# Loads, warm products and the first scale row at the start of a hybrid gMLP, GLA and PEER trunk

## The reference

```python
def rmsnorm(x, g):
    xf = x.astype(jnp.float32)
    y = xf * lax.rsqrt(jnp.mean(xf * xf, axis=-1, keepdims=True) + NORM_EPS)
    return (y * g.astype(jnp.float32)).astype(x.dtype)

def mixer_a(h, w_in, b_in, ln_g, ln_b, w_s, b_s, w_out):
    z = jax.nn.gelu(h @ w_in + b_in, approximate=False)   # w_in: 1024 x 4096
    ...
```

## Time and profile before

| | |
|---|---|
| Median of 3 runs | 1977.58 us (1977.37 to 1978.27) |
| The profiled execution | 1977.18 us |
| Its span in the profile | 1975.5 us |
| TensorE busy | 1939.1 us (98%) |
| VectorE busy | 1348.2 us (68%) |
| ScalarE busy | 1071.4 us (54%) |
| GpSimd busy | 271.4 us (14%) |
| Memory traffic | 338.82 MB, mean 172 GB/s |

### The profile page before, as it was taken

One profiled execution on the slowest core, in us unless ns is written; L12 is line 12 of the kernel. 1 busy time (PEld: TensorE's weight loads), 2 busy tenths in 40 slices (PEclk: granted clock), 3 DMA queues, 4 the chain that ended last, 5 costly groups with the idle time before them and its releaser, 6 DMA issues.

```text
span 1975.5 us, 39160 instructions
## 1 busy us (share of the span) xinstructions
PE 1939.1 (98%) x12636; PEld 1768.9 (90%) x12636; DVE 1348.2 (68%) x2319; ACT 1071.4 (54%) x1864; POOL 271.4 (14%) x122
## 2 busy tenths in 40 slices
PE   7989999999999999999999999999999999999998
PEld 6878999999999888888888799999999998888887
DVE  5774859478888666666658649575888876666666
ACT  4535444566666555445565544445666665544554
POOL 0113770200000000000006068420000000000000
PEclk9999999999999999999999999999999999999999
DMA  7744455544444555555554344555444445555554
GB/s 259 240 138 153 150 188 181 182 158 138 138 138 139 191 191 193 194 195 192 191 167 133 127 151 163 184 185 181 139 138 138 140 158 192 193 193 195 194 191 149
DMA packets 92806, 338.82 MB, mean 172 GB/s; under 512 B 10384, under 2 KB 10512, under 8 KB 92240
## 3 DMA queue, kind: packets, MB, share of 16 engines
q1 hardware_dynamic: 90864, 329.49, 50.0%
q0 software_dynamic: 1888, 8.62, 1.3%
HBM read 337.02 MB, written 1.05 MB: 171 GB/s over the span
## 4 chain that ended last, share of the span: by engine, by line
PE 87%; POOL 4%; issue 4%; DVE 3%; ACT 1%; DMA 0%; POOLq 0%; DVEq 0%; ACTq 0%
PE psum L1079 86%; POOL tile_lo L369 4%; DVE tile_lo L702 1%; ACT tile_hi L440 1%; DVE zv L803 0%; DVE qe L1017 0%; DMA gain_row<-in_gains 0%; DVE zu L812 0%; DVE ke L1018 0%; ACT hT_hi L475 0%; DVE hn L752 0%; DVE zu L777 0%; DVE score_in L1029 0%; DVE x L736 0%; DVE yT_lo L818 0%
## 5 line engine op out<-in xcount | busy, mean ns | idle before, releaser
L702 DVE TENSOR_TENSOR tile_lo<-raw,tile_hi 128x1024 fp32r<-128x1024 f32 x548 | 676.6, 1235 | 295.0 <-ACT tile_hi L440 294.6
L440 ACT ACTIVATE tile_hi<-raw 128x1024 fp32r<-128x1024 f32 x624 | 655.5, 1051 | 349.5 <-PE psum L1079 348.9
L1079 PE MATMUL psum<-hT_hi,tile_hi 128*128 128x256 f32 x2368 | 591.3, 289 | 3.8 <-ACT hT_hi L475 2.7
L1079 PE MATMUL psum<-hT_lo,tile_hi 128*128 128x256 f32 x2368 | 577.2, 283 | 0.0
L1079 PEld LDWEIGHTS psum<-hT_hi,tile_hi 128*128 128x128 f32 x2368 | 451.2, 191 | 5.8 <-ACT hT_hi L475 3.4
L1079 PEld LDWEIGHTS psum<-hT_lo,tile_hi 128*128 128x128 f32 x2368 | 451.9, 191 | 0.0
L1079 PE MATMUL psum<-hT_hi,tile_lo 128*128 128x256 f32 x2368 | 332.9, 283 | 3.7 <-POOL tile_lo L369 3.7
L1079 PEld LDWEIGHTS psum<-hT_hi,tile_lo 128*128 128x128 f32 x2368 | 305.3, 192 | 4.9 <-POOL tile_lo L369 4.9
L580 ACT ACTIVATE w_hi<-acts 128x256 fp32r (+1 forms) x256 | 106.8, 418 | 341.7 <-PE psum L1079 341.0
L1079 PE MATMUL psum<-tile_lo,w_hi 128*128 128x512 f32 x1024 | 274.9, 389 | 0.0
L1079 PE MATMUL psum<-tile_hi,w_lo 128*128 128x512 f32 x1024 | 274.7, 389 | 0.0
(11 more groups left out here) (184 smaller groups left out, 1365.4 us busy)
## 6 DMA issues: line engine op xcount, KB each, us to landing
raw<-in_u SPq DMA_DIRECT2D x256, 512.0 KB, 3.3
raw<-in_v SPq DMA_DIRECT2D x256, 512.0 KB, 3.3
raw<-in_a_in SPq DMA_DIRECT2D x32, 512.0 KB, 4.5
raw<-in_w_q SPq DMA_DIRECT2D x32, 512.0 KB, 3.3
raw<-in_a_out SPq DMA_DIRECT2D x16, 512.0 KB, 3.2
raw<-in_b_rv SPq DMA_DIRECT2D x16, 512.0 KB, 3.3
raw<-in_b_qk SPq DMA_DIRECT2D x8, 512.0 KB, 3.2
raw<-in_b_out SPq DMA_DIRECT2D x8, 512.0 KB, 3.3
```

The costliest lines, as they stand in the source:

```text
L440: act.activation(tile_hi[slot % SPLIT_SLOTS][:, :], raw[slot][:, :], ACT.Copy).then_inc(hi_ready, 1)
L702: dve.tensor_tensor(tile_lo[s][:, :], raw[slot][:, :], tile_hi[s][:, :].bitcast(F32), ALU.subtract).then_inc(lo_ready, 1)
L1079: return pe.matmul(o, a, b, start=start, stop=stop, skip_group_check=True)
```

## The change

It has four parts. The request for the first gain row moves from GpSimd to ScalarE, ahead of its norm. SyncE waits until both halves of x have landed before it requests tiles 0 and 1, requests tile 2 when tile 0 has landed, and tile 3 when tile 1 has. GpSimd, in the place of the gain row, fills the block from which warm products read with zeros. TensorE, before it waits for the constants, runs 72 products of this block with itself into a PSUM bank that is used later.

```diff
@@ -75,6 +75,7 @@
 RAW_SLOTS = 4
 SPLIT_SLOTS = 2
 WARM = 28
+WARM_FIRST = 72
 LOWEST = -3.0e38
 
 
@@ -226,6 +227,7 @@
         raw_loaded = [sem(f"raw_loaded{s}") for s in range(RAW_SLOTS)]
         hi_ready, lo_ready, tile_used = sem("hi_ready"), sem("lo_ready"), sem("tile_used")
         numbers_ready = sem("numbers_ready")
+        warm_ready = sem("warm_ready")
         consts_loaded = sem("consts_loaded")
         x_loaded = [sem(f"x_loaded{h}") for h in range(TT)]
         gain_loaded = [sem(f"gain_loaded{i}") for i in range(5)]
@@ -311,7 +313,11 @@
                         sp.wait_ge(made, i * RAW_SLOTS + (count + s - start))
                         load(t[name][i * RAW_SLOTS + s], s)
 
+            for h in range(TT):
+                sp.wait_ge(x_loaded[h], 16)
             for s in range(RAW_SLOTS):
+                if s >= SPLIT_SLOTS:
+                    sp.wait_ge(raw_loaded[s - SPLIT_SLOTS], 16)
                 load(t["a_in"][s], s)
             stage("a_in", AIN, RAW_SLOTS, N_AIN)
             stage("a_out", AOUT, 0, N_AOUT)
@@ -344,7 +350,7 @@
                     pool.wait_ge(free, count)
                 pool.dma_start(gain_row[:, :], t["gains"][i].partition_broadcast(P)).then_inc(gain_loaded[i], 16)
 
-            load_gain(0, None, 0)
+            pool.memset(numbers16[:, 0:P // GROUP, :], 0.0).then_inc(warm_ready, 1)
 
             pool.wait_ge(hn_ready[0], 1)
             pool.dma_start(b_in[:, 0:A_WIDTH], t["b_in"][0:A_WIDTH].partition_broadcast(P)).then_inc(b_in_loaded[0], 16)
@@ -476,6 +482,7 @@
                                    psum[:, 4 + b, :].rearrange("p (a b) -> p a b", a=4), ACT.Copy).then_inc(hT_hi_ready[i], 1)
 
 
+            act.dma_start(gain_row[:, :], t["gains"][0].partition_broadcast(P)).then_inc(gain_loaded[0], 16)
             norm(0, 0, 1)
 
             def a_gelu(j, h):
@@ -1174,6 +1181,9 @@
 
 
             warm = numbers16[:, 0:P // GROUP, :].rearrange("p a b -> p (a b)")
+            pe.wait_ge(warm_ready, 1)
+            for c in range(WARM_FIRST):
+                product(psum[:, 4, 0:P], warm, warm, start=True, stop=True)
             pe.wait_ge(consts_loaded, 16)
             norm(0)
             for j in range(A_BLOCKS):
```

## The result

The changed kernel takes 1980.87 us (median of 18 executions, 1978.98 to 1983.8), the kernel before in the same series 1978.32 (18 executions, 1977.33 to 1979.9): +2.55 us, a ratio of 1.0014 with a 95% interval of 1.0007 to 1.002. The interval leaves out 1, so the change is slower, but by less than the 0.2% that the prediction set as its bound for no change. The profiled execution took 1979.51 us, with a span of 1977.8 (before 1975.5).

A forecast was written before the change was run, and what follows sets the result against it. The prediction took TensorE's stream as bound, its start set by gain row and weight tile 1's landing. Conversion 1 0.86 us later, other parts 0, summed to +0.9 us: 1978.5 us by the median, range 1975.6 to 1981.1.

The forecast's parts named there:

- the 0.2% that the prediction set as its bound for no change: Whole kernel: a measurement can tell about 0.2%, 4.0 us, from no change; chance of staying within it 0.91.
- The start is bound twice: Before the product stream: gain row and weight tile 1's landing both bind, without slack; removing the 1.95 us gain-row wait leaves the other.
- The second x was to lie 1.5 us later: Start transfers: sharing engines with the gain row delays second x by 1.3 to 1.8 us, middle 1.5, to 7.0 us.
- Tile 0 was to land 3.2 us after its request: First weight tile on SyncE's queue: requested at 7.05 us, landing 3.2 us later as a tile alone does, at 10.25.
- The 1.3 us from tile 0 to tile 1: Weight transfers: tile 1's bytes follow tile 0's, so it lands 1.3 us later, at 11.55 us.
- the rival 5%: TensorE idles before first products, stays at 1.2 GHz into the stream, 2.7 us more a tile; 1983.9 us; chance 5%.
- Against: the first products of before came after a 4.4 us run of work begun cold and were already quick: Stream's start on TensorE: argument against the rival of a slower clock, which cost 2.7 us a tile; chance 5%.
- The 72 products were hidden: TensorE before the transposes: warm products take 4.5 to 8.9 us, covered; value taken 0, bounds 0 to 0.2 us gained.
- b_in had 0 in the sum: GpSimd's bias-row transfer beside tile 1: counted 0; rival 1.3 to 2.6 us more, 1979.8 to 1981.1 us, chance 13%.
- x near 7.0: Sign in the profile after: the second x lands near 7.0 us, not 5.5.
- conversion 1 near 11.5: Sign in the profile after: ScalarE's conversion of weight tile 1 begins at its landing, near 11.5 us.
- the stream at 16.0: Sign on TensorE: the stream of products begins near 16.0 us instead of 15.18, later stretches the same, shifted.

The follow-up runs named there:

- e1: Kernel before with only the first gain row's request moved to ScalarE's queue, no waits or warm products; 0.35 us under before.
- e12: Kernel before, reordered only: ScalarE converts tile 1 after the four copies, VectorE makes the low halves first; 1977.94 us, 0.42 under before.
- e10: Changed kernel with b_in's first half requested later and TensorE kept busy by 100 first products and 50 before tile 0; 2.61 us over before.
- e6: Changed kernel without SyncE's waits ahead of the first four weight tiles; 0.24 us over before.
- e8: Kernel before with e12's order of work and the first gain row requested on SyncE's queue behind x; 1977.33 us, 1.36 under before.
- e2: Kernel before with only SyncE's waits ahead of the first four weight tiles added; 1.34 us over before.
- e4: Changed kernel without GpSimd's memset and the 72 warm products; 2.47 us over before.
- e5: Changed kernel with 100 instead of 72 first products and 44 more between the last transpose and tile 0; 2.53 us over before.
- e7: Changed kernel with the gain row requested on SyncE's queue behind x and ahead of the constants; 1.77 us over before.
- e9: Changed kernel with the first half of bias row b_in requested after ScalarE has converted tile 1; 2.58 us over before.
- e3: Kernel before with only GpSimd's memset and the 72 warm products added; 0.19 us under before.
- e11: Kernel e8 with GpSimd's memset and the 72 warm products added; 1978.37 us, 0.19 over before.

## Why the prediction was right, and where its sizes were off

*The bound.* "The start is bound twice" held, and it is the step that mattered: e1 took the gain row off the chain and won nothing, and with tile 1 off the path e12 had the gain row as its bound. It is not a clean test, since in e1 x came later and scaling began when it had before; no run has the gain row early, x at 5.5 us and the tiles requested at once.

*The mechanism.* Sharing, later request, pause, later tile 1: each link was seen in its place. The sign and the outcome within 0.2% held; the size was 0.9 us against 1.77 from transfers and 2.55 in the medians. Of the 2.4 us between 1978.5 and 1980.87, 0.7 are the starting point: the kernel before took 1978.32 in this series, not 1977.58. Its spread was 2.6 us too, not half a microsecond. Two terms of the transfers were too small. The second x was to lie 1.5 us later, and was 2.0 (7.47): both bounds, 1.3 and 1.8, were under it. The Trainium skill (Trainium Kernel Development and Optimization, Key Constraints) says that the queues interleave, and the trace agrees, 96 packets to 90; but taking turns explains 0.52 MB at the 396 GB/s of 5 to 7 us, 1.3 us. A further part is the slow start, 94 GB/s from 2 to 3 us for 225: some 0.13 MB less, an estimate of 0.3 us. What makes up the rest stays open. Tile 0 was to land 3.2 us after its request, the figure of a tile alone in mid-kernel, and took 3.7. The 1.3 us from tile 0 to tile 1 were right (1.2). In sum 11.55 became 12.44.

*The clock.* The sum gave it nothing and the rival 5%, at 2.7 us a tile and in its full size. The profile shows it in the changed kernel for 0.5 us, and in five other profiled kernels with the waits for 0.9 to 2.8; only e10's has none. The step that failed is "Against: the first products of before came after a 4.4 us run of work begun cold and were already quick": that run was 3.7 us of transposes and 0.6 us without work, so it showed what the clock does after 0.6 us, and the change makes 3.0 of it. The profiles bear the gap out. Ahead of the first product TensorE was idle for 0 to 1.3 us in before, e1, e6, e8, e10 and e12, and none of them shows a fall near it; it was idle for 1.9 to 3.0 us in the changed kernel, e2, e4, e5, e7 and e9, and all six do. e3 and e11 were idle for 2.3 and 2.6 us between the warm products and the transposes, and fell among the transposes. It is one execution of each, and no run varied the gap alone.

The clock is a cost of some executions more than others: executions over 1982 us were 5 of 18 of the changed kernel and, of 11 each, 3 of e2, 4 of e4, 2 of e5, 2 of e7, 4 of e9 and 1 of e10; of the other 65 of e1, e3, e6, e8, e11 and e12 (all but the one of 10227 us), and of 126 of before, none. Only one of those over 1982 was profiled, e2's: its 5.6 us over before's profile are 0.7 of transfers, 2.8 of the clock at the start, and most of the rest the later fall described below. That the others are of the same kind is argued and not shown.

*At nothing.* The 72 products were hidden, the transposes got quicker (eight in 1.23 us), and nobody gained: e4 against the changed kernel. b_in had 0 in the sum: e9 bears it out within 0.3 us, while between the filled kernels, with b_in and without (e5, e10), it is 0.9 (13.82 against 12.92).

*What would show it.* x near 7.0, conversion 1 near 11.5 and the stream at 16.0 were named, and 7.47, 12.46 and 16.95 came.

## What to carry to other kernels

When a wait ends last, look for what ends just before it: here two bounds lay within 0.1 us of each other, and an edit that removed one and delayed x won nothing. Holding back a transfer until another has landed puts its whole latency behind that event and can leave the engines idle (0.23 in use from 7 to 9 us here). An early request behind the urgent one on the same queue cost the urgent one nothing: x landed at 5.5 us with four tiles requested behind it, and at 5.56 with none (e2). And two harmless edits can meet: the shared engines only cost once a wait had been tied to the transfer that they slowed.

## What the runs showed of the hardware that was not expected

How fast the transfers begin goes with the queue that carries the gain row. From 2 to 3 us the seven profiles in which ScalarE's queue has it (changed, e1, e4, e5, e6, e9, e10) moved 70 to 115 GB/s, the other seven 225 to 324, those among them too in which the same row goes on SyncE's queue behind x (e7, e8, e11: 279 each). Why that is so stays open.

The granted clock's column shows 1.00 at the start of every execution, while the first transposes, without warm products, take 1.73 us for seven, and in the changed kernel, behind them, 1.23 us for eight: before its first change in an execution the column does not tell the level.

The clock also falls far from the change. At 119 to 124 us, in the gap ahead of the mixer's output product, e8's profile and e12's (columns as in the earlier trace rows):

```profile
119.00:124.00 5.00, 4.39 (x19) 3.66 (x20) 3.13 (x6) 1.06 (x1) 0.00 (x0) 1.00 0.01 3
```

```profile
119.00:124.00 5.00, 4.13 (x11) 3.29 (x12) 3.21 (x6) 0.00 (x0) 0.00 (x0) 0.66 0.01 3
```

From `yT_lo` to the first product with the keys it is then 59.4 us instead of 57.7 (176.7 - 117.3 against 174.8 - 117.1), 1.7 us for what is the same program text from there on. In e8 the profiled execution took 1977.21 us, in e12 1979.0. The profiles of e2, e6, e7, e10 and e11 have this fall too. The executions of the kernel before lie in two heaps, about 1977 and about 1979 us; that this fall is what parts them is argued from these profiles and not shown. The Trainium skill (TensorE: Matmul & The Clock Gate, Part 1) says that the point at which sustained products bring the quicker level varies from run to run. These runs agree: the same 72 warm products, begun at 1.07 us, took 5.77 us in the changed kernel's profile and 6.79 in e9's, which has the same TensorE program. The fall came at different times too, at 14.7 and at 13.4 us.
